# TensorE multiplies constants in front of eighteen waits at stage borders

## What is computed

```python
for li in range(DEPTH):
    mod = c_act @ w_ada[li] + b_ada[li]
    m = unpack(modulate(rms_norm(x, norm1_w[li]), sh1, sc1) @ w_in[li], lb_all[li])
    ...
    x = x + g1 * merge(att, rec, four, w_out[li], dt)
    x = x + g2 * conv_ffn(modulate(rms_norm(x, norm2_w[li]), sh2, sc2),
                          w_up[li], conv_w[li], conv_b[li], w_down[li])
```

## Time and profile before

| | |
|---|---|
| median of 3 runs | 1936.63 us (1935.42 to 1941.82) |
| the profiled execution | 1933.17 us |
| its span, first to last instruction | 1931.3 us |
| mean granted TensorE clock | 0.965 of 2.4 GHz |
| TensorE busy, matmuls | 1784.3 us (92%) |
| VectorE, ScalarE, GpSimd busy | 1038.0, 847.8, 91.5 us |
| HBM traffic | 257.84 MB read, 134 GB/s over the span |

### The profile page before, as it was taken

The page is one execution under the profiler, slowest core; times in us unless marked ns, Lnnn a source line. Parts: engine busy times, 40 slices in busy tenths (PEclk is TensorE's granted clock), DMA queues, the critical chain, the costliest instruction groups (busy, mean ns, idle before and its releaser), DMA issues.

```text
span 1931.3 us, 27373 instructions
## 1 busy us (share of the span) xinstructions
PE 1784.3 (92%) x11292; PEld 1492.5 (77%) x11292; DVE 1038.0 (54%) x1456; ACT 847.8 (44%) x1223; POOL 91.5 (5%) x171
## 2 busy tenths in 40 slices
PE   5999988799999999988998789987999899999998
PEld 3777766577777778876777579966999879889877
DVE  1333377654444453552737557756665665454475
ACT  2342455433333343354454345544343345565563
POOL 0000012210000000010001100001000010000010
PEclk9999999899999999989998889988999999999999
DMA  9553100034455432244210365543566465555562
GB/s 300 205 183 131 66 1 2 23 109 148 158 175 172 154 110 81 94 136 148 84 53 1 106 201 175 186 152 120 175 191 182 153 191 169 175 167 164 178 113 68
DMA packets 211594, 260.74 MB, mean 135 GB/s; under 512 B 4673, under 2 KB 173299, under 8 KB 211215
## 3 DMA queue, kind: packets, MB, share of 16 engines
q1 hardware_dynamic: 207850, 247.69, 39.9%
q0 software_dynamic: 3232, 11.15, 2.8%
q10 hardware_dynamic: 389, 0.15, 0.0%
HBM read 257.84 MB, written 1.12 MB: 134 GB/s over the span
## 4 chain that ended last, share of the span: by engine, by line
PE 76%; DVE 9%; ACT 5%; DMA 4%; issue 2%; SPq 2%; POOL 1%; DVEq 0%; ACTq 0%; POOLq 0%
PE acc L714 22%; PE acc L716 21%; PE acc L715 21%; PE acc L755 2%; DMA weights<-in_w_in_dram 2%; DVE weights_low L1884 2%; DVE scratch L2063 1%; ACT weights_high L1440 1%; PE acc L967 1%; PE acc L1186 1%; SPq L1272 1%; POOL small L1322 1%; DMA weights<-in_w_down_dram 1%; DMA weights<-in_w_up_dram 1%; ACT mixer_scratch L1672 1%
## 5 line engine op out<-in xcount | busy, mean ns | idle before, releaser
L1884 DVE TENSOR_TENSOR weights_low<-weights,weights_high 128x2048 fp32r<-128x2048 f32 (+1 forms) x184 | 416.9, 2268 | 575.0 <-ACT weights_high L1440 574.9
L1440 ACT ACTIVATE weights_high<-weights 128x2048 fp32r<-128x2048 f32 (+1 forms) x184 | 348.3, 1896 | 641.4 <-DMA weights<-in_w_up_dram 190.2
L714 PE MATMUL acc<-normed_t_high,weights_high 128*128 128x256 f32 (+1 forms) x1824 | 581.1, 319 | 11.4 <-DVE weights_low L1884 10.4
L716 PE MATMUL acc<-normed_t_high,weights_low 128*128 128x256 f32 (+1 forms) x1824 | 567.6, 311 | 0.0
L715 PE MATMUL acc<-normed_t_low,weights_high 128*128 128x256 f32 (+1 forms) x1824 | 567.4, 311 | 0.0
L714 PEld LDWEIGHTS acc<-normed_t_high,weights_high 128*128 128x128 f32 x1824 | 348.8, 191 | 39.5 <-DVE weights_low L1884 12.4
L715 PEld LDWEIGHTS acc<-normed_t_low,weights_high 128*128 128x128 f32 x1824 | 347.2, 190 | 24.6 <-issue 4.3
L716 PEld LDWEIGHTS acc<-normed_t_high,weights_low 128*128 128x128 f32 x1824 | 346.9, 190 | 21.3
L714 PE MATMUL acc<-weights_high,normed_t_high 128*128 128x512 f32 (+1 forms) x792 | 314.8, 397 | 30.9 <-DVE normed_t_low L2207 26.0
L715 PE MATMUL acc<-weights_low,normed_t_high 128*128 128x512 f32 (+1 forms) x792 | 309.8, 391 | 0.0
L716 PE MATMUL acc<-weights_high,normed_t_low 128*128 128x512 f32 (+1 forms) x792 | 309.7, 391 | 0.0
(11 more groups left out here) (245 smaller groups left out, 1761.4 us busy)
## 6 DMA issues: line engine op xcount, KB each, us to landing
weights<-in_w_up_dram SPq DMA_DIRECT2D x44, 1024.0 KB, 7.2
weights<-in_attn_w_in_dram SPq DMA_DIRECT2D x40, 1024.0 KB, 5.2
weights<-in_w_ada_dram SPq DMA_DIRECT2D x38, 1024.0 KB, 5.4
weights<-in_conv_w_in_dram SPq DMA_DIRECT2D x32, 1024.0 KB, 5.8
weights<-in_w_in_dram SPq DMA_DIRECT2D x24, 1024.0 KB, 7.3
weights<-in_w_down_dram SPq DMA_DIRECT2D x20, 1024.0 KB, 5.1
arena<-in_w_ada_dram SPq DMA_DIRECT2D x8, 1024.0 KB, 9.9
weights<-in_w_out_dram SPq DMA_DIRECT2D x8, 1024.0 KB, 5.0
```

Source lines behind the costliest of these rows:

```text
L714: pe.matmul(o, ah, bh, start=start, stop=False)
L716: return pe.matmul(o, al, bh, start=False, stop=stop)
L1440: act.activation(hi_slot(n)[:, 0:used], slot(n)[:, 0:used], ACT.Copy).then_inc(hi_in.sem, 1)
L1884: dve.tensor_tensor(slot(n, ring_lo)[:, 0:used], slot(n)[:, 0:used], hi_slot(n)[:, 0:used], ALU.subtract).then_inc(lo_in.sem, 1)
```

## The change

The change adds a table of places with a number for each, and a function that writes that many matmuls of 128x256 into the bank that the next `open_group` of the same pool will look at. The bank is not taken, so whoever opens it next writes over it from the start. Before the first of the matmuls TensorE waits for the bank, as `open_group` does after it. Operands are the identity (stationary) and columns 0 to 255 of the constants (moving), both float32. No other engine's list changes.

```diff
+        BUSY = {("norm", "n2", 0): 5, ("norm", "n1", 1): 5, ("norm", "n2", 1): 6, ("norm", "cn", 0): 20, ("norm", "an", 0): 2,
+                ("w_out", 0): 7, ("w_out", 1): 4, ("w_down", 0): 8, ("w_down", 1): 14, ("c_out",): 11,
+                ("w_in", 1, "qa", 1): 3, ("w_in", 1, "ka", 0): 7, ("w_in", 1, "va", 0): 7, ("w_up", 1, 0, 1): 8,
+                "first scores": 7, "last heads": 3, "last attention": 3}
...
+            def keep_busy(place, pool_=EVERY):
+
+                n = BUSY.get(place, 0)
+                if not n:
+                    return
+                b = pool_[turn[pool_] % len(pool_)]
+                if uses[b]:
+                    pe.wait_ge(taken[b], uses[b])
+                for i in range(n):
+                    pe.matmul(ps[:, b, 0:256], ident, wide[:, 0:256], start=(i == 0), stop=(i == n - 1))
+
             def weights(key):
 
+                keep_busy(key)
                 n = read[0]
...
             def norm(N):
                 first = True
+                keep_busy(("norm", *N))
                 for k in range(KT):
...
                 gates(0)
+                keep_busy("first scores")
                 for i in range(8):
                     scores(i)
...
                         u = st - 3
+                        if u >= U - 2:
+                            keep_busy("last heads")
                         pe.wait_ge(o_done.sem, o_done.after((li, u)))
...
             def w_out(li):
                 live = range(NT) if li == 0 else range(2, NT)
+                keep_busy(("w_out", li))
...
             def rows_out(name, parts, live, c_of, total):
 
+                keep_busy(name)
                 for c in range(2):
...
+            keep_busy("last attention", SCORES)
             pe.wait_ge(q_done.sem, q_done.after(QKEYS[-1]))
```

## The result

The change took a median of 1927.38 us (1919.6 to 1933.67, 9 runs) where the kernel before took 1935.8 us (1933.47 to 1941.82, 9 runs). The ratio is 0.9941, 95% interval 0.9925 to 0.9962 over the two times it was measured (0.9925 to 0.9957 the first time). The ratio is the one on record, over the runs of both kernels, and not the quotient of the two medians, which is 0.9957. So the change is faster by 8 us by the medians and by 11 by the ratio, where 20 were forecast. The forecast was 1916.3; the result lies in the range, near its slow end.

What follows compares the result with a forecast made beforehand. The prediction took TensorE, busy 92% of the span and partly at its low clock, as the bound. 29.0 us won less 8.7 cost gave 20.3, so 1936.6 became 1916.3 us, range 1907 to 1931.

Steps and rivals of the forecast that it cites:

- The third rival: Everywhere filled: constants, nearly all zeros, do not hold the clock; 1950.9 us or more, chance 0.08.
- The first rival: At the norms: the clock still falls despite the constants, 20.74 us of work staying slow; 1925.8 us, chance 0.13.
- Won: 29.0 us: Filled slow stretches: the clock holds, so TensorE's work there runs faster; 29.0 us won, bounds 19.5 and 33.0.
- the 1.0 taken off at the scores: After layer 0's first scores: 1.0 us deducted from the 4.7 gain, since VectorE feeds the next scores with little idle time.
- Where the constants stand in nobody's wait: Five places (va, w_up, first scores of layer 1, last attention, last heads) where constants cost time, 8.7 us in all.
- va, +2.9: Layer 1 values: seven constants need the bank being waited for, so they start after the wait; 2.9 us lost.
- w_up, +1.7: Layer 1, w_up: eight constants stand one item before the wait and delay the next weights load; 1.7 us, bounds 0 and 3.4.
- First scores of layer 1, +2.0: Between two gate groups: constants delay the second group and attention's first scores; 2.0 us, bounds 1.1 and 2.5.
- Last attention and last heads, 2.1 together: Three constants before a last-attention product that waits for nothing, 1.3 us; fillings at the last heads, 0.8 us.
- What is late next: Weight splits: just in time in layer 1's w_in and w_up, well ahead in layer 0's products and the second block.
- the first two rivals: Norm borders stay slow: 1925.8 us, chance 0.13; splits of weights become the bound: 1925 us, chance 0.11.
- There they end some 0.6 us ahead of the data, and cost nothing: In front of w_down of layer 1 and norm cn, and alike places: constants fit inside the waits, at no cost.

Runs made afterwards that it cites:

- e8: The change with half as many constants at every place, rounded up; ratio 0.9968 to the kernel before.
- e1: The change without the eight constants before the second item of w_up in layer 1; 1924.03 us, ratio 0.9909 to the kernel before.
- e5: The change itself, run a second time as a control; 1928.05 us, ratio 0.9943 to the kernel before.
- e7: The change without constants at va, w_up's second item and layer 1's first scores; constants added at last key rotation, ka, w_up group 1, c_in; ratio 0.9884 to before.
- e2: The change without the seven constants before va of layer 1; 1924.01 us, ratio 0.9917 to the kernel before.
- e6: The change without constants at va, w_up and the first scores of layer 1; 1922.0 us, ratio 0.9922 to the kernel before.
- e12: The change with va's seven constants moved before the last key rotation and eleven instead of seven before ka; ratio 0.991 to the kernel before.
- e4: The kernel before with one filling only, eight constants before the second item of w_up in layer 1; 1936.79 us, ratio 0.9988.
- e11: e7 with the eight constants before the second item of w_up put back; 1917.22 us, ratio 0.9872 to the kernel before.
- e3: The change without constants at va, w_up, first scores of layer 1, last heads and last attention; 1928.31 us, ratio 0.9938 to the kernel before.
- e10: e7 again, unchanged, as a control; 1917.62 us, ratio 0.9873 to the kernel before.
- e9: e7 with seven more places filled, at attention's transposes, layer 1's first real scores and behind ada's gate rows; 1914.81 us, ratio 0.9871 to the kernel before.

## Why the prediction was right in sign and 11 us off in size

- **The clock mechanism: right.** The mean clock went to 0.983 (forecast about 0.98). The low clock is gone behind w_down, cn, w_out, c_out and the first scores of layer 0. The third rival, constants of zeros that hold nothing, is refuted: twenty of them at cn took 8.79 us and the clock stood at 1.00 behind them, where the rival had fifteen of them take 12.6, and in e8 half the number let it fall. The first rival had a rule of the Trainium skill beside it (TensorE: Matmul & The Clock Gate, Part 4: PE-mode transpose), that the high clock does not engage for transposes. At cn the trace of the change disagrees once more: its transposes begin at 1338.35, and the clock is at 1.00 until 1350. But the rule is for a matmul in transpose mode, and the records, all named MATMUL, don't tell whether that mode was on. Of the four norm stretches that this rival wanted to keep (20.74 us), three are gone and one is half there: 2.94 us of slow work at 834.7, in the norm n1 of layer 1, where 5.89 stood. It fell there again in e1, e5, e7 and others, and not in e2, e6 and e12.
- **"Won: 29.0 us": too much by 4.** Own work fell by 25.3 us. Three things stood against the forecast. Behind waits for weights there are 16.3 us of slow PE work (the four rows above), worth 7.5; the forecast had left 6.6 of such work (3.20 and, among, 3.41), so this is 4.5 worse. The norm n1 kept 2.9, worth 1.4. And the recurrence of layer 0 has 10.3 us at 254 and 298, worth 4.7, of which the profile of before has none; as the last section shows, this differs between executions of the same instructions, so the 4.7 is chance. Some came back: the fall at 1843 of the earlier trace rows is gone (2.4), the stretch at va holds constants in place of products (1.6), and the 1.0 taken off at the scores was not lost. That sum gives 23.4; the other 2 us stay unexplained.
- **"Where the constants stand in nobody's wait", 8.7 us: the step that failed, by 10.6 us** (19.3 measured). By its terms:
  - va, +2.9: the mechanism was right (the bank's own wait stays, the constants follow it), but I priced the constants at the high clock, in a place where I had just said that the clock falls. Measured 4.08 + 4.42 - 3.72 = 4.8. The term contradicted the sentence beside it.
  - w_up, +1.7: 3.4 of constants, and four waits that change: 4.34 to 0.69, 2.69 (before a later item's ada matmul, as in e4) to 0, new ones of 4.51 and 3.10. Sum +4.6 in this execution, of which e1, the same without these constants, keeps 1.0 (8.1 us of waits for 7.0). So by the traces 3.6 of it goes with the filling and 1.0 with a PE that came early; alone, in e4, the filling added 0.9. In the time of the whole neither e4 nor e11 shows a cost. How much of the 4.6 is the filling's price stays open, between nothing and 4.
  - First scores of layer 1, +2.0: 0.43 to 3.10, 2.7. Last attention and last heads, 2.1 together: about 3. Both were fairly priced. Left out of account was that the constants at the last heads also hold the clock (e3).
- **"What is late next", the splits of weights: named, priced as a rival of all or nothing, and left out of the sum.** It came in part, and at places that I had charged with nothing. ka's wait of 3.67 us was filled with 3.2 and still had 2.42 left. In c_in a wait of 2.10 is new: I had written that in the second block these splits are made well ahead. They are not: ScalarE starts the high halves behind its evictions of the norm, 4.3 us before the product both before (1349.28, product at 1353.57) and now (1345.20, 1349.49); by the traces a PE at the low clock only took long enough to hide that, which no run tried by itself. The wait repeats in e5 and e12 (2.08 and 2.10); the fall behind it does not. The row of the change:

```profile
1345.20 3.70 ACT L1464 ACTIVATE weights_high<-weights 128x2048 fp32r<-128x2048 f32 x2
```
```profile
1349.49 0.39 PE L731 MATMUL acc<-normed_t_high,weights_high 128*128 128x256 f32 x1 [2.10 <-DVE weights_low L1908]
```

  In all, waits for the low halves of weights went from 11.5 to 15.0 us, though a filling stands in front of two of the old ones. ka, c_in and what w_up measured above its term are 1.9 + 2.1 + 2.9 = 6.9 of the 10.6 us; of the 2.9 it is open whether they belong here or to the filling. This rival's time of 1925 was in the end nearer than the forecast, and the result lies in the range because the range took in the first two rivals.
- **"There they end some 0.6 us ahead of the data, and cost nothing": nearly.** At the twelve fitted places idle time and constants together grew by 0.2 us or less each (at cn 0.41 + 8.79 against 9.03), 1.6 us in all. With the five places, ka and c_in that makes 20.6; waits elsewhere that became 1.3 us shorter make it the 19.3.
- **Expected at va, "the whole wait of 3.7 us still there"**: seen. **At w_up "a wait of about 1 us before (1, 0) and a new one before (1, 1)"**: seen, 0.69 and 4.51.

Shown by runs: that the fillings win time, and that the win goes with the clock (the change, e5; half of both in e8); that w_up's filling alone changes the time by less than can be measured (e4); that the set of moves in e7, the first scores of layer 1 left alone among them, gives another 0.6% (e7 and e10 against the change and e5). Argued from traces only: which of these moves gives how much, and how the 19.3 us divide over the places, since one execution stands behind each figure and the intervals of e1, e2 and e12 each overlap the change's.

## What to carry to other kernels

Price a PE that runs faster against the chain that feeds it, item by item: every product that a low clock had delayed past its data is a wait to come, and each such wait can lose the clock again. Put filler work in front of a wait in a bank that is already free, since filler that asks for the very bank of the wait begins when the wait is over. A filling has to cover most of the wait: rests of 0.4 to 0.8 us kept the clock at nearly every place, rests of 4.3 and 4.7 lost it, and rests of 2.0 to 2.5 went either way (lost at ka with 2.42, kept at va in e7 with 2.25). Half of each filling bought half of the gain. Filling ever more places (e9) ended in equal time: what it won in own work came back as idle time and constants.

## What the hardware showed that I had not expected

Multiplications by an identity, nearly all zeros, keep the granted clock at 1.00 for 8.8 us with nothing else on PE (cn). The falls are not a fixed property of a kernel's instructions. In the recurrence of layer 0, whose instructions are the same in all these kernels, the window of 245 to 345 us reads, for the kernel before, for e4 (equal to it up to there), for e7 and for e10 (equal to e7 throughout):

```profile
245.00:345.00 100.00, 85.73 (x813) 1.00 0.02 6
```
```profile
245.00:345.00 100.00, 88.78 (x795) 0.93 0.00 1
```
```profile
245.00:345.00 100.00, 88.66 (x774) 0.93 0.04 12
```
```profile
245.00:345.00 100.00, 90.14 (x728) 0.86 0.01 1
```

Over all fourteen profiles the clock of this window goes from 0.86 to 1.00, and only before's is at 1.00. Here, where PE has many short waits, the clock falls in one execution and not in the next; from 0.93 to 0.86 is 13.6 us more of slow work, worth 6.3. A reader who compares two profiles of such a kernel should leave that much to chance before naming a cause, or read the falls of both first.
